# Gate matrices of a PEER layer as one fp32r product per token, and value products of 256 columns

## The reference

```
q = (xt @ w_pq).reshape(T, 8, 2, 128)
s = einsum('thpd,hpkd->thpk', q, sub_keys)           # 128 scores for each of 2 halves
s1, i1 = top_k(s[:, :, 0], 16);  s2, i2 = top_k(s[:, :, 1], 16)
top_s, top_pos = top_k(s1[..., :, None] + s2[..., None, :], 16)
experts = i1 * 128 + i2 at top_pos;  gates = softmax(top_s)
act = gelu(einsum('tkd,td->tk', u[experts], x));  y = einsum('tk,tkd->td', gates * act, v[experts])
```

## Time and profile before

| | |
|---|---|
| median of 3 runs | 2162.21 us (2161.71 to 2163.72) |
| profiled execution | 2161.53 us, span 2159.7 us |
| PE busy | 2074.5 us, 96% |
| PEld | 1855.7 us |
| DVE, ACT, POOL | 1134.1, 904.6, 1092.3 us |

### The profile page before, as it was taken

The page is one execution under the profiler, slowest core; times in us unless marked ns, Lnnn a source line. Parts: engine busy times, 40 slices in busy tenths (PEclk is TensorE's granted clock), DMA queues, the critical chain, the costliest instruction groups (busy, mean ns, idle before and its releaser), DMA issues.

```text
span 2159.7 us, 36922 instructions
## 1 busy us (share of the span) xinstructions
PE 2074.5 (96%) x13326; PEld 1855.7 (86%) x13326; DVE 1134.1 (53%) x1819; ACT 904.6 (42%) x1132; POOL 1092.3 (51%) x450
## 2 busy tenths in 40 slices
PE   8797898997999999999999999999999999999996
PEld 6686787886999999999999999988888888888885
DVE  7578547034535990456666664034455445544545
ACT  6332335463543444533333333444444444444443
POOL 6675666874897888877777777860000000000001
PEclk9898999998999999999999999999999999999998
DMA  8443545663665666655555555676666666666663
GB/s 314 123 150 117 165 147 166 186 192 101 205 186 166 195 194 192 189 172 160 163 164 159 162 165 166 185 248 190 185 186 191 186 186 188 189 185 187 190 186 117
DMA packets 104754, 383.32 MB, mean 177 GB/s; under 512 B 12144, under 2 KB 12656, under 8 KB 103408
## 3 DMA queue, kind: packets, MB, share of 16 engines
q1 hardware_dynamic: 101232, 365.50, 54.9%
q10 hardware_dynamic: 3456, 16.89, 2.2%
HBM read 378.15 MB, written 4.19 MB: 177 GB/s over the span
## 4 chain that ended last, share of the span: by engine, by line
PE 71%; POOL 16%; issue 11%; DVE 1%; POOLq 0%; ACT 0%; DVEq 0%; ACTq 0%
PE ps L1209 23%; PE ps L1211 23%; PE ps L1210 23%; POOL wlo L360 16%; PE ps L1492 2%; PE ps L1465 0%; POOLq L359 0%; DVE x_back L1164 0%; DVE stats L631 0%; ACT big L605 0%; DVE stats L1175 0%; DVE big L1169 0%; ACT x_back L612 0%; POOLq L363 0%; PE ps L1518 0%
## 5 line engine op out<-in xcount | busy, mean ns | idle before, releaser
L360 POOL TENSOR_TENSOR wlo<-raw,whi 128x1024 fp32r<-128x1024 f32 x444 | 1086.5, 2451 | 355.6 <-ACT whi L410 351.4
L410 ACT ACTIVATE whi<-raw 128x1024 fp32r<-128x1024 f32 x436 | 462.4, 1062 | 808.3 <-PE ps L1211 807.0
L1209 PE MATMUL ps<-xh,whi 128*128 128x256 f32 x2176 | 618.7, 284 | 0.7 <-POOL wlo L360 0.7
L1210 PE MATMUL ps<-xl,whi 128*128 128x256 f32 x2176 | 607.3, 279 | 0.0
L1211 PE MATMUL ps<-xh,wlo 128*128 128x256 f32 x2176 | 607.2, 279 | 0.0
L1136 DVE TENSOR_TENSOR wlo<-raw,whi 128x1024 fp32r<-128x1024 f32 x248 | 304.0, 1226 | 350.1 <-ACT whi L563 350.1
L563 ACT ACTIVATE whi<-raw 128x1024 fp32r<-128x1024 f32 x256 | 271.8, 1062 | 403.7 <-PE ps L1211 403.7
L1210 PEld LDWEIGHTS ps<-xl,whi 128*128 128x128 f32 x2176 | 414.1, 190 | 0.1
L1209 PEld LDWEIGHTS ps<-xh,whi 128*128 128x128 f32 x2176 | 408.9, 188 | 1.1 <-issue 1.1
L1211 PEld LDWEIGHTS ps<-xh,wlo 128*128 128x128 f32 x2176 | 408.4, 188 | 0.0
L1209 PE MATMUL ps<-whi,gate_hi 128*128 128x512 f32 x1024 | 406.9, 397 | 0.0
(11 more groups left out here) (194 smaller groups left out, 1780.2 us busy)
## 6 DMA issues: line engine op xcount, KB each, us to landing
raw<-in_w_u SPq DMA_DIRECT2D x256, 512.0 KB, 3.6
raw<-in_w_v SPq DMA_DIRECT2D x256, 512.0 KB, 4.2
raw<-in_w_front SPq DMA_DIRECT2D x180, 512.0 KB, 3.6
big<-in_x_t ACTq DMA_DIRECT2D x4, 512.0 KB, 9.2
big<-in_x ACTq DMA_DIRECT2D x4, 512.0 KB, 5.1
big<-in_mem ACTq DMA_DIRECT2D x4, 512.0 KB, 6.7
big<-in_mem_t ACTq DMA_DIRECT2D x2, 1024.0 KB, 6.7
big<-in_x ACTq DMA_DIRECT2D x2, 1024.0 KB, 8.0
```

The lines of the kernel that those rows point to most:

```text
L360: nc.gpsimd.tensor_tensor(wlo[:, j % SPL, :], raw[:, j % RAW, :], whi[:, j % SPL, :], ALU.subtract).then_inc(lo_done, 1)
L410: nc.scalar.activation(whi[:, j % SPL, :], raw[:, j % RAW, :], ACT.Copy).then_inc(hi_done, 1)
L1209: nc.tensor.matmul(out_ap, sh, mh, start=start, stop=False)
L1210: nc.tensor.matmul(out_ap, sh, ml, start=False, stop=False)
```

## The change

The two one-hots change roles and type. The one-hot of the first index is the stationary operand (`hot1_row`, 128 columns, fp32r, single buffer). The one-hot of the second index is scaled by the gate, in two parts instead of three: the value rounded to fp32r and the rest (`hot2_rows`, fp32r, double buffer). The two parts lie side by side, so a token takes one matmul of 256 columns, two a pair, each with its own start and stop, and a pair fills a whole bank. DVE adds the two halves with a `reduce_sum` from bank 4 or 5 into bank 7, and the multiplication into W reads bank 7 after a wait for that sum. The tables are made in one pass rather than three. In V, four column quarters of 256 take the place of two halves of 512; 24 matmuls a piece with 24 weight loads, where one half-bank opens the bank for both. The filler tile `rest_of_gates` grows by 384 float32 values, which moves `xh`, `xl`, `x2_back` and `last_gain` up by 1536 bytes a partition.

```diff
-        i1_table = of_u.enter_context(nc.sbuf_tensor("i1_table", [P, T], F32))
-        hot2_row = of_u.enter_context(nc.sbuf_tensor("hot2_row", [P, 2, P], BF16))
-        hot1_rows = of_u.enter_context(nc.sbuf_tensor("hot1_rows", [P, 2, 2, 3, P], BF16))
+        i2_table = of_u.enter_context(nc.sbuf_tensor("i2_table", [P, T], F32))
+        hot1_row = of_u.enter_context(nc.sbuf_tensor("hot1_row", [P, 2, P], F32R))
+        hot2_rows = of_u.enter_context(nc.sbuf_tensor("hot2_rows", [P, 2, 2, 2, P], F32R))
...
-        sb("rest_of_gates", [P, 128])
+        sb("rest_of_gates", [P, 512])
...
+            high = hot2_rows[:, 0].rearrange("p a b c -> p (a b c)")[:, 0:T]
             step(nc.vector.tensor_copy(rest, ps[:, 5, 0:T]))
...
+            step(nc.vector.tensor_copy(high, rest))
+            nc.vector.tensor_copy(parts_table[:, 0, :], high)
+            step(nc.vector.tensor_tensor(parts_table[:, 1, :], rest, high, ALU.subtract))
...
+            def hot_i2(g, q):
                 for m in range(2):
                     t = bass.ds(g * 2 + m, 1)
+                    parts = parts_table[:, :, t].broadcast_to([P, 2, P])
+                    ins = nc.vector.scalar_tensor_tensor(hot2_rows[:, q, m], iota[:, :].unsqueeze(1).broadcast_to([P, 2, P]),
+                                                         i2_table[:, t], parts, ALU.is_equal, ALU.mult)
+                ins.then_inc(hot2, 1)
+            def hot_i1(g):
+                nc.vector.tensor_tensor(hot1_row[:, :, :], iota[:, :].unsqueeze(1).broadcast_to([P, 2, P]),
+                                        i1_table[:, bass.ds(g * 2, 2)].unsqueeze(2).broadcast_to([P, 2, P]),
+                                        ALU.is_equal).then_inc(hot1, 1)
...
                 if last > j + 1:
-                    hot_i2(g + 1)
+                    hot_i1(g + 1)
+                gates = ps[:, 7, j % 2 * T:(j % 2 + 1) * T].rearrange("p (m k) -> p m k", m=2)
+                nc.vector.reduce_sum(gates, ps[:, 4 + j % 2, :].rearrange("p (m h k) -> p m k h", m=2, h=2), AX).then_inc(joined_parts, 1)
...
                 dve.wait_ge(act_taken, i * CHUNKS_PER_BODY + (C_ONES + 1 + j // 2))
+                dve.wait_ge(joined_parts, g + 1)
                 w = W[:, :, bass.ds(g * 2, 2)]
-                nc.vector.tensor_tensor(w, ps[:, 4 + j % 2, 0:T].rearrange("p (m k) -> p k m", m=2), w, ALU.mult).then_inc(gated, 1)
+                nc.vector.tensor_tensor(w, gates.rearrange("p m k -> p k m"), w, ALU.mult).then_inc(gated, 1)
                 if last > j + 2:
-                    hot_i1(g + 2, j % 2)
+                    hot_i2(g + 2, j % 2)
...
                 for m in range(2):
-                    for part in range(3):
-                        ins = nc.tensor.matmul(ps[:, 4 + j % 2, m * P:(m + 1) * P], hot1_rows[:, j % 2, m, part, :],
-                                               hot2_row[:, m, :], start=part == 0, stop=part == 2)
+                    ins = nc.tensor.matmul(ps[:, 4 + j % 2, m * 2 * P:(m + 1) * 2 * P], hot1_row[:, m, :],
+                                           hot2_rows[:, j % 2, m].rearrange("p a b -> p (a b)"), start=True, stop=True)
...
             def v_products(s, g, half, tb, first=False, last=False):
-                for c in range(2):
-                    t = slice(tb * P, (tb + 1) * P)
-                    cols = slice(c * 512, (c + 1) * 512)
-                    ins = three(ps[:, 4 * tb + 2 * half + c, :], gate_hi[:, g, t], gate_lo[:, g, t], whi[:, s, cols],
-                                wlo[:, s, cols], first, last)
+                t = slice(tb * P, (tb + 1) * P)
+                for c in range(4):
+                    cols = slice(c * 256, (c + 1) * 256)
+                    out = ps[:, 4 * tb + 2 * half + c // 2, c % 2 * 256:(c % 2 + 1) * 256]
+                    opens = first and c % 2 == 0
+                    nc.tensor.matmul(out, gate_hi[:, g, t], whi[:, s, cols], start=opens, stop=False, skip_group_check=True)
+                    nc.tensor.matmul(out, gate_hi[:, g, t], wlo[:, s, cols], start=False, stop=False, skip_group_check=True)
+                    ins = nc.tensor.matmul(out, gate_lo[:, g, t], whi[:, s, cols], start=False, stop=last, skip_group_check=True)
                 return ins
```

More of the change, by code:

```diff
@@ L191, in hymba_layer @@
         ps = ctx.enter_context(nc.psum_tensor("ps", [P, 8, 512], F32))
-        i2_table = ps[:, 3, T:2 * T]
+        i1_table = ps[:, 3, 0:T]
         x2_inverse = ps[:, 2, 0:T]
-        parts_table = ps[:, 6:8, :].rearrange("p a b -> p (a b)")[:, 0:3 * T].rearrange("p (a b) -> p a b", a=3)
+        parts_table = ps[:, 6, :].rearrange("p (a b) -> p a b", a=2)
         def at(off, *dims):
@@ L292, in hymba_layer @@
         hot1, hot2, gate_mat, gated = sem("hot1"), sem("hot2"), sem("gate_mat"), sem("gated")
+        joined_parts = sem("joined_parts")
         ghi_done, glo_done = sem("ghi_done"), sem("glo_done")
@@ L1068, in _ @@
             dve.wait_ge(table_T, 1)
-            nc.vector.tensor_copy(i1_table[:, :], ps[:, 3, 0:T])
-            part, rest = at(TK_AT, 2 * T)[:, 0:T // 2].bitcast(BF16), at(TK_AT + T, T)
+            nc.vector.tensor_copy(i2_table[:, :], ps[:, 3, T:2 * T])
+            rest = at(TK_AT + T, T)
+            high = hot2_rows[:, 0].rearrange("p a b c -> p (a b c)")[:, 0:T]
             step(nc.vector.tensor_copy(rest, ps[:, 5, 0:T]))
[L1073 to L1078, removed]
+            step(nc.vector.tensor_copy(high, rest))
@@ L1079, in _ @@
+            nc.vector.tensor_copy(parts_table[:, 0, :], high)
+            step(nc.vector.tensor_tensor(parts_table[:, 1, :], rest, high, ALU.subtract))
             step(nc.vector.memset(W[:, C_FREE:NK, :], 1.0))
-            def hot_i1(g, q):
+            def hot_i2(g, q):
                 for m in range(2):
                     t = bass.ds(g * 2 + m, 1)
[L1087 to L1096, removed]
+                    parts = parts_table[:, :, t].broadcast_to([P, 2, P])
+                    ins = nc.vector.scalar_tensor_tensor(hot2_rows[:, q, m], iota[:, :].unsqueeze(1).broadcast_to([P, 2, P]),
+                                                         i2_table[:, t], parts, ALU.is_equal, ALU.mult)
@@ L1114, in gate_step @@
                 dve.wait_ge(act_taken, i * CHUNKS_PER_BODY + (C_ONES + 1 + j // 2))
+                dve.wait_ge(joined_parts, g + 1)
                 w = W[:, :, bass.ds(g * 2, 2)]
-                nc.vector.tensor_tensor(w, ps[:, 4 + j % 2, 0:T].rearrange("p (m k) -> p k m", m=2), w, ALU.mult).then_inc(gated, 1)
+                nc.vector.tensor_tensor(w, gates.rearrange("p m k -> p k m"), w, ALU.mult).then_inc(gated, 1)
                 if last > j + 2:
-                    hot_i1(g + 2, j % 2)
-            hot_i2(0)
-            hot_i1(0, 0)
-            hot_i1(1, 1)
+                    hot_i2(g + 2, j % 2)
+            hot_i1(0)
+            hot_i2(0, 0)
+            hot_i2(1, 1)
             full = TOK_PAIRS // BODY
```

## The result

The changed kernel takes 2148.3 us (median of 4 runs, 2147.05 to 2149.79) against 2162.6 (4 runs): ratio 0.9934, 95% interval 0.9917 to 0.9951. It is faster by 14.3 us; a saving of 29 was forecast, and the time is inside the stated range of 2102 to 2158. The profiled execution has a span of 2148.0 us.

The account below looks back on a forecast made before the run. PE was taken as the bound, matmul count times pitch; gate step -21.3, U -14.5 and V +7.0 gave -28.8 us, from 2162.2 to 2133.4, stated as 2133. Range 2102 to 2158, the likeliest case's own 2126 to 2138.

Parts of the forecast that it names:

- What bounds the kernel: From 651 us to V's end, time is matmul count times pitch on PE; everything else is hidden.
- stayed covered: Gate steps on DVE: mean 2.57 us against PE's 2.98, so the added sum costs nothing.
- Gate step on PE: Gate stage: 128 steps costing 51.5 us become two fp32r matmuls each, 30.2 us in all: -21.3 us.
- U pitch after 923: U's 3816 matmuls after the first gate step return from 0.1178 to 0.1133 us without bf16: -14.5 us.
- V: V's 6144 matmuls of 256 columns run at 0.1178 us, 723.8 for 716.8 us: +7.0 us.
- The rule of the Trainium skill: Matmuls cost N / 2.4 GHz plus about 2.5 ns: splitting V loses an estimated 7.7 us, U gains nothing.
- (b): Second level isn't bf16's doing: U and V stay at 0.1178, -14.3 us, 2148; chance 0.16.
- (a): V settles at the low level, 0.1133: -56.3 us in all, 2106; chance 0.27.
- (c): V goes to 0.120, U at low or middle level: -15.3 or -0.8 us, 2147 to 2161; chance 0.13.
- (e): DVE sets the gate step at 3.3 us or more: 2165 and up; chance 0.05.
- (d): Level follows tile place; x moves 1536 bytes, so U, gates and V run at 0.120: +23.7, 2186; chance 0.09.
- Range: Whole kernel: 2102 to 2158 us; the likeliest case's own range 2126 to 2138.

Follow-up runs that it names:

- pad kernel (e6): Changed kernel with a 320-byte filler between hot1_row and hot2_rows, nothing else: 2147.1 us, ratio 0.9929.
- e12: Changed kernel with fillers putting hot1_row at 192 and hot2_rows at 384 modulo 512 bytes: 2105.1 us.
- place kernel (e10): Changed kernel with fillers putting hot1_row at 0 and hot2_rows at 192 modulo 512 bytes: 2100.6 us, ratio 0.9717.
- e14: Kernel before the change (bf16 gates, V at 512 columns) with 320 bytes between hot2_row and hot1_rows: 2157.2 us.
- e15: As e12, with xh and xl moved down 192 bytes to 0 modulo 512: 2142.7 us.
- e5: Changed kernel with single disturbances (split, reordered, plain fp32 or 512-column products) in some pieces of U and V: 2147.2 us.
- e7: Changed kernel with V's very first product cut into 128 + 128 columns: 2146.7 us.
- e8: The pad kernel (e6) with the z tiles 192 bytes higher, at 192 modulo 512: 2145.1 us, ratio 0.9927.
- e11: The place kernel (e10) with the z tiles at 192 modulo 512: 2099.4 us, ratio 0.9708.

## Why the prediction was wrong

- **What bounds the kernel**: right. From the start of U to the end of V PE waits for nothing and the time is matmuls times pitch in all sixteen experiments, and DVE, at 693 ns for the sum (0.68 forecast) and 473 for a scaled one-hot (0.48), stayed covered.
- **Gate step on PE**: right. 501.5 - 480.2 = 21.3, as forecast (-21.3). Two gate products cost two more matmuls of the stream and the 0.20 us behind them went.
- **U pitch after 923: this step failed.** "With no bf16 between them, what set the level 0.1178 is gone", -14.5 us; measured 0. The rows showed that the level began with the gate step, and I took the type of its operands for the cause, as it was the most visible difference. The pad kernel (e6), e12 and the place kernel (e10) differ in nothing but fillers, and the first has the second level and the others not. With fp32r gate products, where the stationary and the moving one-hot tile lie to each other is what began it; this was worth 18.7 us in the gate stage (480.2 - 461.5). Whether bf16 has a part of its own stays open, since the one other placing of bf16 tiles (e14) escaped the level only behind every second step. The placing was in the code and in the text (the rival on the moved x tiles speaks of offsets within 512 bytes), but was not applied to the gate tiles themselves. The step's support, x coming down from 0.120 within six matmuls, was a fall from the highest level and said nothing of the second.
- **V**: the value was right (+7.0, measured +6.9), its reason was half right. The row taken, the front's 0.1175, is a stream on the second level; the place kernel has V at 0.1133 with the same operands. The pitch belonged to the level and not, as I reasoned, to the operand order.
- **The rule of the Trainium skill** ("TensorE: Matmul & The Clock Gate", section "Wait — 56ns, not 53.3ns?"): the sum by its figures, an estimated -21.3 + 7.7 = -13.6, came near the measured -14.3, and its +7.7 near V's +6.9. That is luck: no stretch of fp32r matmuls here held a pitch below 0.1133 for 256 columns or 0.2289 for 512, against an estimated 0.1092 and 0.2158 by that rule.
- **Rivals**: (b) was the outcome, at 2148. (a) needed what the forecast needed and more; its 2106 is about what e12 did with one filler (2105.1). (c) and (e) weren't met. (d)'s mechanism is real (e15), its condition wasn't met: 1536 is a multiple of 512.
- **Range**: it held the time because it took in rival (b); the forecast's own range, 2126 to 2138, didn't. The best of the versions here lies below it.

## What to carry over

In a stream that is bound by TensorE, read the pitch by windows: the same instructions on the same tiles can run at different pitches, and where it steps from one to another is the thing to explain. Before the form of an instruction is blamed, move its tiles and change nothing else; here a filler of 320 and one of 192 bytes were worth 47.7 us of 2148 (46.0 of them by stages, 18.7 in the gate stage and 27.3 in V), three times the change itself. A comparison of tile sizes holds only for the level on which it was made: 256 columns against 512 was +6.9 us on one and -6.7 on the other.

## What the runs showed of the hardware that I had not expected

- A dense stream of fp32r matmuls of 256 columns with a weight load each has three pitches at a granted clock of 1.00: 113.3, 117.8 and 120 ns; one of 512 columns two, 228.9 and 233.3.
- With moving and stationary tile at a distance of 0 modulo 512 bytes the pitch is 120 (U in e15, the query stage in all kernels but two); with 192 (U) and with 320 (V) it is 113.3 or 117.8, by the state the stream is in.
- The second level lasts: over 502 us and into V, through loops and waits that are already met. It has been left by a product split in two (128 + 128 and 32 + 224 in U, 128 + 128 in V of e5, but not in e7), by a piece of 512 columns (e5), at the change from U at 120 to V (e15 enters V at 120 and runs it at 113.3), and by a wait (query stage of e8 and e11); the next wait in e8 began it again.
- Why the distance acts, why 320 begins the second level among gate products and keeps the low one in V, and what the state is, stays open. That it is a clash of the two reads from SBUF is a guess that no run here tests.
